# Every fourth expert row summed by VectorE in SBUF, and a new order in stick-breaking

## The chip, the core and the metric

The kernel runs on one core of one Trainium2 chip, as one program. The metric is the device time of one execution in microseconds; beside it stands the profile of one further execution. Five engines work side by side and wait for each other through semaphores: TensorE (PE, its weight loads PEld), VectorE (DVE), ScalarE (ACT), GpSimd (POOL), and SyncE (SP), which here only starts transfers. The gathers are started by POOL.

## The reference

One encoder layer over 1024 tokens of width 1024, float32 throughout. Two of its parts are touched.

Stick-breaking attention, 8 heads of width 64, strictly causal, in blocks of queries:

```python
z = jnp.einsum('bhtd,bhsd->bhts', qh[:, :, start:end], kh[:, :, :end])
mask = jnp.arange(end)[None, :] < jnp.arange(start, end)[:, None]
log_1m = jnp.where(mask, jax.nn.log_sigmoid(-z), 0.0)
suffix = lax.cumsum(log_1m, axis=3, reverse=True) - log_1m
a = jnp.where(mask, jnp.exp(jax.nn.log_sigmoid(z) + suffix), 0.0)
outs.append(jnp.einsum('bhts,bhsd->bhtd', a, vh[:, :, :end]))
```

PEER, a layer of 16384 single-neuron experts, of which each token takes 16 per head for 8 heads, so 128 rows of u and of v per token:

```python
ub = u[eb]
act = jax.nn.gelu(jnp.einsum('thkd,td->thk', ub, xb).astype(jnp.float32), approximate=False)
w = (gb * act).astype(xb.dtype)
return jnp.einsum('thk,thkd->td', w, v_emb[eb])
```

The result of PEER is added to the residual h, and a last RMSNorm gives the output.

## The kernel before

The program is a sequence of phases with barriers between them: input norm and projections, gated linear attention, stick-breaking, output projection, memory attention, key scores, and the expert phase, which takes two thirds of the time. Inside a phase the program is written out engine by engine, so the order of each engine's instructions is that of the code, and semaphores tie the engines together.

**Stick-breaking** (`stick_phase`). A tile is 128 keys by up to 512 queries, for one head. The list `work` says in which order the tiles are done, `(pair of heads, half of the queries, block of keys)`; `rounds` (L871) writes it for one pair, and an entry with -1 belongs to the pair before. Each entry gives two tiles, one per head. A tile on the diagonal has fewer queries and is masked. In iteration `i` the engines work on entries of different age: TensorE makes r for entry i - 2 (L1002, L1006: the suffix sums, by a triangular matrix and the carry), z for entry i (L1017), and the product with v for entry i - 3 (L1032) into `po`, which holds one half of the queries for one pair. ScalarE takes the exp of r for entry i - 2 (L934, into `aw`, shown as tok) and three passes over z of entry i (L941 to L943). VectorE makes the softplus `sps` (L958, shown as heads) and the carry (L976, L978), and four iterations after a pair's last entry of a half it copies `po` out as a high and a low part (L984, L136, into x_t) and so frees it: `o_free`. POOL masks diagonal tiles, `sps` and `aw`, both on L905.

**The expert phase** (`expert_phase`). Eight blocks of 128 tokens, one token per partition, and 128 expert rows per block. Row R is a gather (L1433) of 128 x 8 KB, u and v of one expert per token, into one of `ROWS` = 7 slots. Then VectorE takes the dot product of u with the normalised token (L1660), ScalarE makes the weight by Gelu and gate (L1774, L1775) and a diagonal matrix of it (L1778, 4 slots `dg`), TensorE adds diagonal times v to the PSUM accumulator of the block (L1905, two matmuls of 512 columns), and `row_used` frees the slot for row R + 7. Before a block's first row TensorE puts the residual H into the accumulator by a product with the identity (L1898). After a block's last row, during the first 16 rows of the next, VectorE works the final norm (`finish`, L1546 to L1569) in steps between the dot products, and SP stores the block. Between dot products VectorE also chooses the experts two groups ahead (`select`), and during the first 4 blocks all engines do memory attention and key scores for the second half of the tokens (`later`, by the table of class `Later`).

## Time and profile before

| | us |
|---|---|
| median of 3 runs | 3914.02 |
| lowest, highest | 3913.75, 3915.89 |
| the profiled execution, its own time | 3910.47 |
| span of its trace | 3908.7 |

| engine | busy us | share |
|---|---|---|
| PE | 3189.3 | 82% |
| DVE | 2324.4 | 59% |
| ACT | 1640.7 | 42% |
| POOL | 1596.6 | 41% |

The span is cut into 40 slices of 97.7 us each; a digit is the busy share of a slice in tenths. A row of a timeline gives start, duration, engine and line, what is written from what, and in brackets how long the engine sat idle before it and what it waited for. In a windows row the engines stand in the order PE, PEld, DVE, ACT, POOL, each with its busy time and in brackets the number of instructions, then the granted TensorE clock as a share of full speed, the busy share of the 16 DMA engines and the rate. The median time of the line's transfers "to landing" is from the issue until the data is there. A wait for several things is put down to the last. The shares are averages over phases with different limits.

### The profile page before, as it was taken

The page shows a single profiled execution, that of the slowest core. Times are in us where ns is not written, and L with a number is a line of the kernel's source. Part 1 is how long each engine was busy: PE and PEld are TensorE (multiplying, and loading weights), DVE is VectorE, ACT ScalarE, POOL GpSimd, SP SyncE. Part 2 cuts the span into 40 slices and gives each one's busy share as a digit, 9 for nine tenths or more (in the row PEclk, how much of TensorE's full clock was granted, in tenths as well). Part 3 has the DMA queues.
Part 4 walks back from the last instruction along what each step waited for, and adds up shares of the span by engine and source line. Part 5 has one row for each costly group of instructions (what it writes and reads, how often), then busy time and mean ns, then how long its engine had stood idle before and what let it go on. Part 6 is the DMA issues. An engine that isn't in the chain of part 4 may idle for free.

```text
span 3908.7 us, 35644 instructions
## 1 busy us (share of the span) xinstructions
PE 3189.3 (82%) x10072; PEld 1663.8 (43%) x10072; DVE 2324.4 (59%) x5493; ACT 1640.7 (42%) x4273; POOL 1596.6 (41%) x1176
## 2 busy tenths in 40 slices
PE   6798788977887888888888888888787777877777
PEld 5577533666666443434333444443222222222222
DVE  3343344234334777776776676676667667667665
ACT  2121377223222555544544444454444444444443
POOL 0000011000000556444555445445765766666765
PEclk8899899988988999999999999999999999999999
DMA  2101000221023999999999999999999999999998
GB/s 77 35 24 43 0 1 1 87 97 43 23 76 121 416 409 419 417 415 414 414 414 414 417 410 415 413 408 412 420 414 408 420 405 420 416 415 420 414 407 353
DMA packets 173010, 1147.66 MB, mean 294 GB/s; under 512 B 19472, under 2 KB 21536, under 8 KB 41632
## 3 DMA queue, kind: packets, MB, share of 16 engines
q0 software_dynamic: 147456, 1073.81, 66.8%
q1 hardware_dynamic: 25376, 71.87, 5.1%
q8 instruction: 64, 1.05, 0.1%
q14 instruction: 114, 0.93, 0.1%
HBM read 1141.41 MB, written 4.19 MB: 293 GB/s over the span
## 4 chain that ended last, share of the span: by engine, by line
DMA 29%; POOL 9%; PE 9%; issue 7%; ACT 7%; DVE 6%; POOLq 0%; ACTq 0%; DVEq 0%
DMA expert_rows<-in_uv,expert_index 29%; POOL expert_rows L1433 9%; PE expert_acc L1905 8%; DVE expert_rows L1660 4%; ACT expert_dg L1778 1%; ACT expert_wt L1775 1%; ACT L1774 1%; ACT expert_wt L1774 1%; ACT L1694 1%; DVE expert_w_lo L136 1%; ACT expert_w_hi L131 1%; DVE expert_hot L1523 0%; ACT expert_best L1694 0%; ACT L1720 0%; ACT expert_spare L1720 0%
## 5 line engine op out<-in xcount | busy, mean ns | idle before, releaser
L1905 PE MATMUL expert_acc<-expert_rows,expert_dg 128*128 128x512 f32 x4096 | 2010.6, 623 | 485.4 <-ACT expert_dg L1778 484.6
L1433 POOL DMA_INDIRECT expert_rows<-in_uv,expert_index x1024 | 1547.1, 1511 | 1094.2 <-PE expert_acc L1905 809.1
L1660 DVE CUSTOM_DVE_ANT_0 expert_rows<-expert_rows,expert_xn 128x1024 f32<-128x1024 f32 x1024 | 1254.8, 1225 | 719.5 <-DMA expert_rows<-in_uv,expert_index 716.3
L1905 PEld LDWEIGHTS expert_acc<-expert_rows,expert_dg 128*128 128x128 f32 x4096 | 737.6, 194 | 1606.4 <-ACT expert_dg L1778 1004.9
L1774 ACT ACTIVATE expert_wt<-expert_dot 128x1 f32<-128x1 f32 x1024 | 207.4, 203 | 1329.9 <-DVE expert_dot L1660 1327.6
L1778 ACT ACTIVATE expert_dg<-ident,expert_wt 128x128 f32<-128x128 f32 x1024 | 411.2, 402 | 33.7
L1775 ACT ACTIVATE expert_wt<-expert_wt,expert_gate 128x1 f32<-128x1 f32 x1024 | 301.3, 294 | 33.4
L1425 POOL IOTA expert_iota<- 128x16 f32 x1 | 0.1, 144 | 534.8 <-PEq L1793 534.8
L905 POOL TENSOR_SCALAR_AFFINE_SELECT heads<-heads 128x128 f32<-128x128 f32 x64 | 20.7, 324 | 331.6 <-DVE heads L958 331.3
L958 DVE SCALAR_TENSOR_TENSOR heads<-stick_pz,stick_t 128x512 f32<-128x512 f32 (+3 forms) x96 | 53.2, 557 | 134.0 <-ACT stick_t L943 133.8
L1774 ACT ACT_TABLE_LOAD x79 | 101.4, 1283 | 7.3 <-DVE expert_dot L1660 6.0
L142 PE MATMUL expert_side<-late_hi,expert_w_lo 128*128 128x512 f32 x128 | 103.6, 809 | 0.0
L1002 PE MATMUL stick_pz<-heads,negtri 128*128 128x512 f32 (+3 forms) x192 | 87.4, 545 | 0.9 <-POOL heads L905 0.9
L1660 DVE DVE_READ_ACCUMULATOR2_ANT expert_dot<- 128x1 f32 x1024 | 84.8, 83 | 0.0
L1694 ACT ACT_TABLE_LOAD x62 | 79.5, 1283 | 1.1
L136 DVE TENSOR_TENSOR expert_w_lo<-expert_w_raw,expert_w_hi 128x512 fp32r<-128x512 f32 x48 | 33.2, 693 | 74.5 <-ACT expert_w_hi L131 74.5
L1032 PE MATMUL stick_po<-tok 128*64 128x512 f32 (+3 forms) x192 | 43.7, 535 | 33.4 <-DVE x_t_lo L136 17.8
L1006 PE MATMUL stick_pz<-stick_carry,negone 128*128 128x512 f32 (+3 forms) x160 | 63.6, 481 | 0.0
L934 ACT ACTIVATE tok<-stick_pz 128x512 f32<-128x512 f32 (+3 forms) x96 | 43.6, 481 | 45.2 <-PE stick_pz L1006 44.9
L142 PE MATMUL keys_pq<-z_a_hi,pq_w_lo 128*128 128x512 f32 x128 | 51.9, 406 | 11.2 <-DMA keys_sk<-in_sub_keys 9.3
L487 POOL MEMSET decay_keep<- 128x1024 f32 x1 | 1.0, 951 | 142.1 <-POOLq L334 142.1
L142 PE MATMUL mixout_bank<-out_w_hi,x_t_lo 128*128 128x512 f32 x128 | 51.1, 400 | 7.5 <-DVE out_w_lo L136 7.5
(367 smaller groups left out, 4182.0 us busy)
## 6 DMA issues: line engine op xcount, KB each, us to landing
expert_rows<-in_uv,expert_index POOLq DMA_INDIRECT x1024, 12.4
H<-in_x SPq DMA_DIRECT2D x8, 1024.0 KB, 10.3
pq_w_raw<-in_w_pq SPq DMA_DIRECT2D x16, 512.0 KB, 3.3
expert_w_raw<-in_w_pq SPq DMA_DIRECT2D x32, 256.0 KB, 8.9
stick_w_raw<-in_w_feat SPq DMA_DIRECT2D x8, 512.0 KB, 3.3
tok_w_raw<-in_w_tok SPq DMA_DIRECT2D x8, 512.0 KB, 4.0
out_w_raw<-in_w_out SPq DMA_DIRECT2D x8, 512.0 KB, 5.3
mk_w_raw<-in_w_mk SPq DMA_DIRECT2D x8, 512.0 KB, 5.0
```

The source lines that it names most:

```text
L136: return nc.vector.tensor_tensor(lo, x, hi.bitcast(F32), ALU.subtract)
L142: nc.tensor.matmul(out, wl, xh, start=start, stop=False)
L958: nc.vector.scalar_tensor_tensor(sps[:, s, c0:], pz[s][:, c0:], 0.0, t[:, s, c0:], ALU.max, ALU.add).then_inc(sp_ready, 1)
L1002: last = nc.tensor.matmul(pz[s][:, c0:], negtri[:, :], sps[:, s, c0:], start=False, stop=(c1 == HALF), skip_group_check=True)
L1006: last = nc.tensor.matmul(pz[s][:, c1:], negone[:, :], carry[:, h, th, (k + 1) % 2, c1:], start=False, stop=True, skip_group_check=True)
L1433: pool.indirect_dma_start(out=rows[R % ROWS], out_offset=None, in_=uv, in_offset=bass.IndirectOffsetOnAxis(ap=index[:, q, r:r + 1], axis=0 ...
L1660: nc.vector.tensor_tensor_reduce(rows[R % ROWS][:, 0:D], rows[R % ROWS][:, 0:D], xn[:, :], 1.0, 0.0, ALU.mult, ALU.add, dot[:, h % 2, r:r ...
L1694: nc.scalar.activation(best[:, q, :], best[:, q, :], ACT.Exp, bias=small[:, 0, q:q + 1], accum_out=small[:, 1, q:q + 1]).then_inc(exp_read ...
L1774: link(nc.scalar.activation(wt[:, s, 0, r:r + 1], dot[:, s, r:r + 1], ACT.Gelu))
L1775: link(nc.scalar.activation(wt[:, s, 1, r:r + 1], wt[:, s, 0, r:r + 1], ACT.Copy, scale=gate[:, q, r:r + 1]))
L1778: nc.scalar.activation(dg[:, r % DG, :], co.ident[:, :], ACT.Copy, scale=wt[:, s, 1, r:r + 1]).then_inc(diag_ready, 1)
L1905: last_mm = nc.tensor.matmul(acc[:, h * HALF:(h + 1) * HALF], dg[:, r % DG, :], rows[(TOPK * (PH * b + g) + r) % ROWS][:, D + h * HALF:D + ...
```

## The change

Four edits. In the expert phase every fourth row (R mod 4 = 3, an own row) is no longer multiplied by a diagonal and summed in PSUM. VectorE multiplies it by its weight and adds it to `own_acc`, a buffer in SBUF, one row late: behind the dot product of the next row. The first own row of a block adds to H, so TensorE no longer puts H into the accumulator. POOL waits for `own_used` where the slot held an own row and for `row_used` otherwise, `finish` adds the two sums, and `cand` shares its memory with `hot`. In stick-breaking the entry (-1, 0, 1) moves from second to first place in `rounds`; POOL does the masks of `aw` of an iteration ahead of those of `sps`; and VectorE copies `po` out at the start of its iteration instead of the end.

```diff
--- before.py
+++ after.py
@@ -868,7 +868,7 @@
 
-    rounds = [(0, 1, 7), (-1, 0, 1), (0, 1, 6), (-1, 0, 0), (0, 1, 5), (0, 1, 4), (0, 0, 3), (0, 1, 3), (0, 0, 2),
+    rounds = [(-1, 0, 1), (0, 1, 7), (0, 1, 6), (-1, 0, 0), (0, 1, 5), (0, 1, 4), (0, 0, 3), (0, 1, 3), (0, 0, 2),
               (0, 1, 2), (0, 1, 1), (0, 1, 0)]
@@ -906,14 +906,14 @@
             for i in range(M + 2):
+                for n in (2 * i - 4, 2 * i - 3):
+                    if n >= 0 and diag[n]:
+                        pool.wait_ge(a_ready, n + 1)
+                        strict(aw[:, n % S, :], tile(n)[3], a_masked)
                 for m in (2 * i, 2 * i + 1):
                     if i < M and diag[m]:
                         pool.wait_ge(sp_ready, m + 1)
                         strict(sps[:, m % S, :], tile(m)[3], sp_masked)
-                for n in (2 * i - 4, 2 * i - 3):
-                    if n >= 0 and diag[n]:
-                        pool.wait_ge(a_ready, n + 1)
-                        strict(aw[:, n % S, :], tile(n)[3], a_masked)
 
@@ -948,6 +948,14 @@
             for i in range(M + 5):
+                n = 2 * (i - 4) + 1
+                if 0 <= n < N and tile(n)[2] == 0:
+                    pr, th, _, _ = tile(n)
+                    dve.wait_ge(pv_done, n + 1)
+                    hi, lo = (x[:, GLA_HEADS + pr, th * HALF:(th + 1) * HALF] for x in mix_t)
+                    nc.vector.tensor_copy(hi, po[th][:, :]).then_inc(hi_ready, 1)
+                    dve.wait_ge(hi_ready, ended.index((pr, th)) + 1)
+                    low(nc, lo, po[th][:, :], hi).then_inc(o_free, 1)
                 two = (2 * i, 2 * i + 1) if i < M else ()
@@ -976,14 +984,6 @@
                             nc.vector.tensor_copy(new[:, c0:c1], sps[:, s, c0:c1]).then_inc(carry_ready, 1)
-                n = 2 * (i - 4) + 1
-                if 0 <= n < N and tile(n)[2] == 0:
-                    pr, th, _, _ = tile(n)
-                    dve.wait_ge(pv_done, n + 1)
-                    hi, lo = (x[:, GLA_HEADS + pr, th * HALF:(th + 1) * HALF] for x in mix_t)
-                    nc.vector.tensor_copy(hi, po[th][:, :]).then_inc(hi_ready, 1)
-                    dve.wait_ge(hi_ready, ended.index((pr, th)) + 1)
-                    low(nc, lo, po[th][:, :], hi).then_inc(o_free, 1)
 
@@ -1296,6 +1296,21 @@
     E = 2 * D
+    OWN = 4
+
+    def own(R):
+
+        return R % OWN == OWN - 1
+
+    def own_rows(R):
+
+        return (R + 1) // OWN
+
+    def pe_rows(R):
+
+        return R + 1 - own_rows(R)
+
+    own_ready, own_used = sem("own_ready"), sem("own_used")
     landed = [sem(f"landed{j}") for j in range(ROWS)]
...
@@ -1541,13 +1560,14 @@
                 ms, var, tmp, y = (small2[:, j:j + 1] for j in range(4))
-                dve.wait_ge(row_used, TOPK * PH * (b + 1) + ROWS)
+                dve.wait_ge(row_used, pe_rows(TOPK * PH * (b + 1) - 1))
+                dve.wait_ge(own_used, own_rows(TOPK * PH * (b + 1) - 1))
                 dve.wait_ge(stored, 16 * (b + 1))
-                n = put(nc.vector.tensor_copy(hb[:, :], acc[:, :]))
+                n = put(nc.vector.tensor_tensor(hb[:, :], own_acc[:, :], acc[:, :], ALU.add))
                 yield
                 yield
                 have(n)
-                n = put(nc.vector.tensor_tensor_reduce(hb[:, :], hb[:, :], acc[:, :], 1.0, 0.0, ALU.mult, ALU.add, ms))
+                n = put(nc.vector.tensor_tensor_reduce(acc[:, :], hb[:, :], hb[:, :], 1.0, 0.0, ALU.mult, ALU.add, ms))
                 yield
...
@@ -1637,6 +1657,19 @@
 
+            def add_own(R):
+
+                b, r = divmod(R, TOPK * PH)
+                n = own_rows(R)
+                dve.wait_ge(own_ready, n)
+                if r > OWN:
+                    dve.wait_ge(own_used, n - 1)
+                    so_far = own_acc[:, :]
+                else:
+                    so_far = co.H[:, b, :]
+                nc.vector.scalar_tensor_tensor(own_acc[:, :], rows[R % ROWS][:, D:E], wt[:, R // TOPK % 2, 1, R % TOPK:R % TOPK + 1],
+                                               so_far, ALU.mult, ALU.add).then_inc(own_used, 1)
+
             def body(b, odd, more, last):
@@ -1659,6 +1692,8 @@
                                                        ALU.mult, ALU.add, dot[:, h % 2, r:r + 1]).then_inc(dots, 1)
+                        if R and own(R - 1):
+                            add_own(R - 1)
                         later(R)
...
@@ -1772,12 +1808,19 @@
                         link(nc.scalar.activation(wt[:, s, 0, r:r + 1], dot[:, s, r:r + 1], ACT.Gelu))
-                        link(nc.scalar.activation(wt[:, s, 1, r:r + 1], wt[:, s, 0, r:r + 1], ACT.Copy,
-                                                  scale=gate[:, q, r:r + 1]))
-                        act.wait_ge(row_used, TOPK * g + r + 1 + ROWS - DG)
-                        nc.scalar.activation(dg[:, r % DG, :], co.ident[:, :], ACT.Copy,
-                                             scale=wt[:, s, 1, r:r + 1]).then_inc(diag_ready, 1)
-                        later(TOPK * g + r)
+                        R = TOPK * g + r
+                        weight = nc.scalar.activation(wt[:, s, 1, r:r + 1], wt[:, s, 0, r:r + 1], ACT.Copy,
+                                                      scale=gate[:, q, r:r + 1])
+                        if own(R):
+                            weight.then_inc(own_ready, 1)
+                        else:
+                            link(weight)
+                            n = pe_rows(R) - 1
+                            if n >= DG:
+                                act.wait_ge(row_used, n - DG + 1)
+                            nc.scalar.activation(dg[:, n % DG, :], co.ident[:, :], ACT.Copy,
+                                                 scale=wt[:, s, 1, r:r + 1]).then_inc(diag_ready, 1)
+                        later(R)
 
...
@@ -1892,21 +1933,18 @@
                     pe.wait_ge(out_ready, b - 1)
-                if b == HB:
-                    pe.wait_ge(mo_added, 2 * HB)
-                for h in range(2):
-                    nc.tensor.matmul(acc[:, h * HALF:(h + 1) * HALF], co.ident[:, :],
-                                     co.H[:, ds(b, 1), h * HALF:(h + 1) * HALF].rearrange("p o d -> p (o d)"),
-                                     start=True, stop=False, skip_group_check=True)
                 for g in range(PH):
                     for r in range(TOPK):
-                        pe.wait_ge(diag_ready, TOPK * PH * b + (TOPK * g + r + 1))
-                        for h in range(2):
-                            last_mm = nc.tensor.matmul(acc[:, h * HALF:(h + 1) * HALF], dg[:, r % DG, :],
-                                                       rows[(TOPK * (PH * b + g) + r) % ROWS][:, D + h * HALF:D + (h + 1) * HALF],
-                                                       start=False, stop=False, skip_group_check=True)
-                        last_mm.then_inc(row_used, 1)
-                        later(TOPK * (PH * b + g) + r)
+                        R = TOPK * (PH * b + g) + r
+                        if not own(R):
+                            n = pe_rows(R) - 1
+                            pe.wait_ge(diag_ready, n + 1)
+                            for h in range(2):
+                                last_mm = nc.tensor.matmul(acc[:, h * HALF:(h + 1) * HALF], dg[:, n % DG, :],
+                                                           rows[R % ROWS][:, D + h * HALF:D + (h + 1) * HALF],
+                                                           start=not (g or r), stop=False, skip_group_check=True)
+                            last_mm.then_inc(row_used, 1)
+                        later(R)
```

VectorE where head pair 1 follows pair 0 in stick-breaking, before (CAST and the TENSOR_TENSOR behind it are the copy of `po`):

```order
L976 TENSOR_TENSOR stick_carry<-stick_carry,heads 128x128 [waits stick_carry_ready,stick_sp_masked,stick_r_full]
L978 COPY stick_carry<-heads 128x128
L958 SCALAR_TENSOR_TENSOR heads<-stick_pz,stick_t 128x512 [waits stick_logs,stick_carry_ready] x2
L984 CAST x_t_hi<-stick_po 128x512 [waits stick_pv_done]
L136 TENSOR_TENSOR x_t_lo<-stick_po,x_t_hi 128x512 [waits stick_hi_ready]
L958 SCALAR_TENSOR_TENSOR heads<-stick_pz,stick_t 128x384 [waits stick_logs,stick_carry_ready] x2
L976 TENSOR_TENSOR stick_carry<-stick_carry,heads 128x256 [waits stick_carry_ready,stick_sp_masked,stick_r_full]
```

and now:

```order
L984 TENSOR_TENSOR stick_carry<-stick_carry,heads 128x128 [waits stick_carry_ready,stick_sp_masked,stick_r_full]
L986 COPY stick_carry<-heads 128x128
L956 CAST x_t_hi<-stick_po 128x512 [waits stick_pv_done]
L136 TENSOR_TENSOR x_t_lo<-stick_po,x_t_hi 128x512 [waits stick_hi_ready]
L966 SCALAR_TENSOR_TENSOR heads<-stick_pz,stick_t 128x512 [waits stick_logs,stick_carry_ready] x2
L966 SCALAR_TENSOR_TENSOR heads<-stick_pz,stick_t 128x384 [waits stick_logs,stick_carry_ready] x2
L984 TENSOR_TENSOR stick_carry<-stick_carry,heads 128x256 [waits stick_carry_ready,stick_sp_masked,stick_r_full]
```

The copy stands ahead of the iteration's softplus instead of behind it; the lines are numbered 8 higher, and L956 is the old L984.

TensorE at the same place, before; the row that waits for stick_o_free is the new pair's first product into `po`:

```order
L1032 MATMUL stick_po<-tok 64x512 [waits stick_a_ready]
L1032 MATMUL stick_po<-tok 64x512
L1002 MATMUL stick_pz<-heads,negtri 128x384 [waits stick_sp_masked]
L1006 MATMUL stick_pz<-stick_carry,negone 128x256 [waits stick_carry_ready]
L1002 MATMUL stick_pz<-heads,negtri 128x384 [waits stick_sp_masked]
L1006 MATMUL stick_pz<-stick_carry,negone 128x256 [waits stick_carry_ready]
L1017 MATMUL stick_pz<-H 128x512 [waits stick_a_ready]
L1017 MATMUL stick_pz<-H 128x512
L1032 MATMUL stick_po<-tok 64x128 [waits stick_a_masked,stick_o_free]
L1032 MATMUL stick_po<-tok 64x128
```

and now:

```order
L1017 MATMUL stick_pz<-H 128x512 [waits stick_a_ready]
L1017 MATMUL stick_pz<-H 128x512
L1032 MATMUL stick_po<-tok 64x384 [waits stick_a_masked]
L1032 MATMUL stick_po<-tok 64x384
L1002 MATMUL stick_pz<-heads,negtri 128x256 [waits stick_sp_masked]
L1006 MATMUL stick_pz<-stick_carry,negone 128x128 [waits stick_carry_ready]
L1002 MATMUL stick_pz<-heads,negtri 128x256 [waits stick_sp_masked]
L1006 MATMUL stick_pz<-stick_carry,negone 128x128 [waits stick_carry_ready]
L1017 MATMUL stick_pz<-H 128x384 [waits stick_a_ready]
L1017 MATMUL stick_pz<-H 128x384
L1032 MATMUL stick_po<-tok 64x128 [waits stick_a_masked,stick_o_free]
L1032 MATMUL stick_po<-tok 64x128
```

Two products stand where one stood between the last of pair 0 (64x512) and the one that waits: that of the diagonal tile (0, 0, 1), 64x384, has gone ahead.

POOL's first masks of the phase, before (heads is `sps`, tok is `aw`):

```order
L905 AFFINE_SELECT heads<-heads 128x128 [waits stick_sp_ready] x6
L905 AFFINE_SELECT tok<-tok 128x128 [waits stick_a_ready] x2
L905 AFFINE_SELECT heads<-heads 128x128 [waits stick_sp_ready] x2
L905 AFFINE_SELECT tok<-tok 128x128 [waits stick_a_ready] x2
L905 AFFINE_SELECT heads<-heads 128x128 [waits stick_sp_ready] x2
L905 AFFINE_SELECT tok<-tok 128x128 [waits stick_a_ready] x4
```

and now:

```order
L905 AFFINE_SELECT heads<-heads 128x128 [waits stick_sp_ready] x4
L905 AFFINE_SELECT tok<-tok 128x128 [waits stick_a_ready] x2
L905 AFFINE_SELECT heads<-heads 128x128 [waits stick_sp_ready] x2
L905 AFFINE_SELECT tok<-tok 128x128 [waits stick_a_ready] x2
L905 AFFINE_SELECT heads<-heads 128x128 [waits stick_sp_ready] x2
L905 AFFINE_SELECT tok<-tok 128x128 [waits stick_a_ready] x2
```

The masks of `aw` come one iteration's pair earlier among those of `sps`.

VectorE in the expert phase, the middle of a group of rows, before (ISA is the dot product, in two parts):

```order
L1501 MAX expert_best<-expert_cand_rest 128x8
L1502 TENSOR_SCALAR expert_small<-expert_best 128x1
L1660 ISA expert_rows,expert_dot<-expert_rows,expert_xn 128x1024
L1660 ISA expert_dot 128x1
L1505 MAX_INDEX expert_best_j<-expert_best,expert_cand_rest 128x8
L1660 ISA expert_rows,expert_dot<-expert_rows,expert_xn 128x1024
L1660 ISA expert_dot 128x1
```

and now at the same step of the selection:

```order
L1693 ISA expert_rows,expert_dot<-expert_rows,expert_xn 128x1024
L1693 ISA expert_dot 128x1
L1670 SCALAR_TENSOR_TENSOR expert_own_acc<-expert_rows,expert_wt,expert_own_acc 128x1024
L1520 MAX expert_best<-expert_hot 128x8
L1521 TENSOR_SCALAR expert_small<-expert_best 128x1
L1693 ISA expert_rows,expert_dot<-expert_rows,expert_xn 128x1024
L1693 ISA expert_dot 128x1
L1524 MAX_INDEX expert_best_j<-expert_best,expert_hot 128x8
L1693 ISA expert_rows,expert_dot<-expert_rows,expert_xn 128x1024
```

The addition to own_acc stands behind the dot product of the row after and ahead of the step of the selection.

## Rows read from the trace of the kernel before

**Rows 1.** The page's slices, DMA share in tenths and GB/s, 40 equal slices.

```profile
DMA  2101000221023999999999999999999999999998
GB/s 77 35 24 43 0 1 1 87 97 43 23 76 121 416 409 419 417 415 414 414 414 414 417 410 415 413 408 412 420 414 408 420 405 420 416 415 420 414 407 353
```

**Rows 2.** Windows: stretch, length, busy PE, PEld, DVE, ACT, POOL, clock, DMA, GB/s.

```profile
1800.00:2000.00 200.00, 162.74 (x392) 70.28 (x393) 148.51 (x378) 105.47 (x287) 106.19 (x77) 0.98 1.01 416
3000.00:3200.00 200.00, 156.52 (x319) 54.84 (x317) 134.15 (x346) 86.87 (x262) 142.00 (x80) 0.99 1.01 416
```

**Rows 3.** The gather's line: durations in ns, starts, then issue to landing.

```profile
L1433 POOL DMA_INDIRECT expert_rows<-in_uv,expert_index x1024: 984/1495/2066, 1252.9 to 3883.0; - x171
...
DMA to landing us min/median/max: 6.0/12.4/15.5
```

**Rows 4.** Timeline of DVE at the end: start, duration, instruction, idle before.

```profile
3892.92 1.23 DVE L1660 CUSTOM_DVE_ANT_0 expert_rows<-expert_rows,expert_xn 128x1024 f32<-128x1024 f32 x1 [1.25 <-DMA expert_rows<-in_uv,expert_index]
...
3895.41 1.23 DVE L1660 CUSTOM_DVE_ANT_0 expert_rows<-expert_rows,expert_xn 128x1024 f32<-128x1024 f32 x1 [1.25 <-DMA expert_rows<-in_uv,expert_index]
...
3899.71 1.23 DVE L1546 COPY expert_hb<-expert_acc 128x1024 f32<-128x1024 f32 x1 [3.07 <-PE expert_acc L1905]
```

**Rows 5.** Waits in stick-breaking: us in total, times, longest.

```profile
ACT tok L934 <- PE stick_pz L1006: 44.9, 29, 4.5
...
PE stick_po L1032 <- DVE x_t_lo L136: 17.8, 3, 5.9
...
PE stick_po L1032 <- POOL tok L905: 15.5, 9, 2.7
```

**Rows 6.** Timeline where head pair 1 follows pair 0.

```profile
518.70 1.13 PE L1017 MATMUL stick_pz<-H 64*128 64x512 f32 x4
...
524.29 0.68 DVE L984 CAST x_t_hi<-stick_po 128x512 fp32r<-128x512 f32 x1
...
525.01 0.69 DVE L136 TENSOR_TENSOR x_t_lo<-stick_po,x_t_hi 128x512 fp32r<-128x512 f32 x1
...
525.76 0.69 PE L1032 MATMUL stick_po<-tok 128*64 128x128 f32 x4 [5.93 <-DVE x_t_lo L136]
...
528.13 0.38 ACT L934 ACTIVATE tok<-stick_pz 128x256 f32<-128x256 f32 x1 [4.54 <-PE stick_pz L1006]
```

**Rows 7.** Timeline at a later wait for a mask in the same pair.

```profile
540.11 0.85 ACT L934 ACTIVATE tok<-stick_pz 128x384 f32<-128x384 f32 x2
...
541.06 0.55 POOL L905 TENSOR_SCALAR_AFFINE_SELECT heads<-heads 128x128 f32<-128x128 f32 x1 [1.51 <-DVE heads L958]
...
541.57 0.85 POOL L905 TENSOR_SCALAR_AFFINE_SELECT tok<-tok 128x128 f32<-128x128 f32 x2
...
542.47 1.97 PE L1032 MATMUL stick_po<-tok 128*64 128x512 f32 x4 [2.67 <-POOL tok L905]
```

**Rows 8.** The page's groups: line, count, busy, mean ns, idle before.

```profile
L1905 PE MATMUL expert_acc<-expert_rows,expert_dg 128*128 128x512 f32 x4096 | 2010.6, 623 | 485.4 <-ACT expert_dg L1778 484.6
...
L1774 ACT ACTIVATE expert_wt<-expert_dot 128x1 f32<-128x1 f32 x1024 | 207.4, 203 | 1329.9 <-DVE expert_dot L1660 1327.6
...
L1778 ACT ACTIVATE expert_dg<-ident,expert_wt 128x128 f32<-128x128 f32 x1024 | 411.2, 402 | 33.7
...
L1775 ACT ACTIVATE expert_wt<-expert_wt,expert_gate 128x1 f32<-128x1 f32 x1024 | 301.3, 294 | 33.4
```

**Rows 9.** Groups from 1400 us on: the norm's last operation.

```profile
L1569 DVE SCALAR_TENSOR_TENSOR expert_hb<-expert_acc,expert_small,expert_gfinal 128x1024 f32<-128x1024 f32 x8 | 10.2, 1280 | 0.0
```

**Rows 10.** Waits of DVE over the first 16 rows of block 1.

```profile
DVE expert_rows L1660 <- DMA expert_rows<-in_uv,expert_index: 3.8, 6, 0.9
```

**Rows 11.** Timeline: a gather alone, and one issued during a dot product.

```profile
1255.64 0.99 POOL L1433 DMA_INDIRECT expert_rows<-in_uv,expert_index  x1 [0.30 <-issue]
...
3010.24 1.22 DVE L1660 CUSTOM_DVE_ANT_0 expert_rows<-expert_rows,expert_xn 128x1024 f32<-128x1024 f32 x1 [0.71 <-DMA expert_rows<-in_uv,expert_index]
...
3010.41 1.93 POOL L1433 DMA_INDIRECT expert_rows<-in_uv,expert_index  x1 [0.56 <-issue]
```

20 lines of the change are left out of this document (12 added, 8 removed).

## The prediction

> **What bounds the kernel now.** I read the page's slices first. From about 1250 us to the end the DMA digit is 9 and the GB/s row stands at 405 to 420 [rows 1]. That is the expert phase, two thirds of the span. The windows put numbers on it: 416 GB/s and a DMA share of 1.01 in a stretch that also carries the late attention and key scores (DVE busy 148.5 of 200 us, PE 162.7) and the same 416 GB/s in one that carries only expert rows (DVE 134.2, PE 156.5) [rows 2]. Engine load changes and the rate does not, so no engine sets it.
>
> The chain of waits can mislead here: it runs round the loop gather, dot product, weight, matmul, ring slot, next gather, and gives each a share. The end of the phase tells transfer from loop apart. The last gather is issued at 3883.0 [rows 3]; afterwards no slot matters, and the last dot products still start at 3892.92 and 3895.41, 2.49 us apart, each after 1.25 us of waiting for the DMA [rows 4]. So about five rows stand queued in the DMA, drained at one per 2.49 us; issue to landing is 12.4 us in the median against 6.0 at the least [rows 3]. Between landing and freeing a row needs only some 4.2 us (dot 1.23, weight and diagonal about 1, matmuls 2.0). The ring of 7 has slack: the DMA would starve only if a row came free some 12.4 - 6.0 = 6.4 us later than it does.
>
> The other 1250 us are phases bound by engines. The one touched is stick-breaking, 462 to 712 us. In its waits TensorE stands 17.8 us for x_t_lo in three places, up to 5.9 each, and 15.5 us for POOL's mask of the weights in nine; ScalarE stands 44.9 us for TensorE's r matmul [rows 5].
>
> **The change part by part.** Stick-breaking: output copy and rounds. In rows 6 TensorE starts its z matmul at 518.70 for 1.13 us, then may not write the next head pair's first product into po until VectorE has copied the finished pair out. That copy (0.68 + 0.69 us) stands at the end of VectorE's iteration, behind a softplus that needs three ScalarE passes over the tile whose z was only just made. It begins at 524.29 and TensorE goes on at 525.76: an idle 5.93 us. ScalarE then idles 4.54 us up to 528.13 [rows 6]. Afterwards VectorE copies first, which needs only a product one iteration older, and the tile (0, 0, 1) goes between the finished pair and the first tile of the next, so the buffer is asked for one iteration later. Both remove the same wait, 3 x 5.93 = 17.8 us [rows 5, 6]. The copies (1.37 us) now stand ahead of the softplus, hidden in VectorE's wait for ScalarE.
>
> Stick-breaking: mask order. POOL waits in program order, and the masks of a fresh tile stand ahead of those of weights ready earlier. In rows 7 the second exp ends at 540.96 (540.11 + 0.85), but POOL begins the sps mask at 541.06 and the aw pair at 541.57, which ends 542.42; TensorE goes on at 542.47 after 2.67 idle. Weights first, each mask (0.3 us) follows its exp and the second ends near 541.3: 1.1 us earlier, and the remaining 1.6 us are ScalarE's own. Nine waits at about 1 us give 9 us at most [rows 5, 7].
>
> The ceiling is 17.8 + 9 = 27 us, the floor near zero, because TensorE runs into what is late next: in the widest tiles TensorE and ScalarE are both nearly full, and narrow diagonal tiles leave short iterations where the chain z, three activations, softplus, mask, r needs two iterations. With x_t_lo gone, the next thing late is the exp that ScalarE owes; it had 4.54 us idle there to give, plus smaller gaps, 44.9 us in total [rows 5, 6]. I take the larger term almost whole (16 of 17.8) and half of the smaller (5 of 9): -21 us, with 10 and 27 as ends.
>
> Expert phase, removed: per own row (256 of 1024) four matmul pieces, 2010.6 / 1024 = 1.96 us of TensorE, some 500 of the 2010.6 us of L1905, and one ScalarE diagonal, 0.40 us; also the products that put H into the accumulator [rows 8]. TensorE has time to spare beside a bound DMA, so these are worth 0.
>
> Added: 256 times scalar_tensor_tensor over 128x1024. No row has it with three SBUF operands; with a PSUM input it takes 1.28 us [rows 9], and the dot product with two SBUF inputs 1.23 [rows 4]. I take 1.28, so 328 us of VectorE. In the densest window VectorE is busy 148.5 of 200 us and some 76 rows pass, 19 of them own: 148.5 + 24.3 = 173 of 200 [rows 2]. On average it fits, so 0. The tight place is a block's first 16 rows, where the normalisation of the block before is worked in: from 1588.7 to 1630.6 VectorE waits for landings only 3.8 us [rows 10], and four additions want 5.1. It is 1.3 us short there and catches up in the next group; of the 6.4 us of slack that is a fifth. I charge +1 us for all seven boundaries; had the queue no slack it would be 7 x 1.3 = 9.
>
> Moved: an own row is freed by VectorE after the next row's dot product, so not 4.2 but about 5.0 us after it landed (2.49 + 1.23 + 1.28). The add also waits for ScalarE's weight; that is 0.5 us of work after a dot 2.5 us before, so it is there unless ScalarE is changing tables. POOL waits for two semaphores in turn, with as many gathers as before; SP's transfers are the same. The first DMAs are not touched.
>
> The tail: today 3.07 us lie between the last dot and the copy of acc [rows 4]: 0.20 + 0.29 for the weight [rows 8], then diagonal and matmuls. Row 1023 is an own row, so it becomes 0.2 + 0.29 + 1.28 and four handoffs, about 1.85: -1.2 us. The sum of both halves takes the place of a copy of equal size.
>
> **A port that speaks against the change.** POOL's gather takes 0.98 us at the least and 2.07 at the most [rows 3], and the pattern is plain: the gather at 1255.64, before the first dot product, takes 0.99 and stands 0.30 behind the one before it; the one at 3010.41, issued 0.17 after a dot began at 3010.24, takes 1.93 and so ends 0.9 after the dot ended [rows 11]. A vector instruction with two SBUF operands holds POOL up until it ends. The new add is of that kind, so an own row may hold one gather up once more, by up to 1.28 us. The Trainium skill states the mechanism (SBUF — State Buffer, Who interferes with whom): a VectorE instruction with two SBUF inputs and a GpSimd instruction that reads SBUF exclude each other, and the later one blocks fully. The trace agrees, with 0.99 against 1.93. By the rule alone the sum would be that of rival 2.
>
> **The sum.** The profiled execution has a span of 3908.7 and a time of 3910.47. -21 + 0 + 1 - 1.2 = -21.2, so 3889.3. The median shown is 3914.02, 3.55 above it, which gives 3892.8; I say 3892.
>
> **The rivals.**
> 1. Stick-breaking gives back most of it. For it: ScalarE and TensorE alternate as the bound, and the reordered diagonal tiles stand two in a row, (1, 1, 7) and (1, 1, 6), so that a carry is asked for one iteration after it is made. Against it: both engines idle at the same place. A third of the 21 stays, -7: 3907.
> 2. VectorE or the port slows the expert loop: slower. Place: the gather's issue. Today a gather and its issue time fill about 2.5 us when a dot is in the way. If each own row held POOL 1.25 us more than it can make up, four rows would take 4 x 2.49 + 1.25 = 11.2 us and the phase 256 x 1.25 = 320 more: 4212. It decides once the queue in the DMA is used up, that is after five such rows without a catch-up. Against it: POOL issues a gather in 0.99 + 0.30 = 1.3 us when nothing is in the way [rows 11], so one unblocked gather in four repays one blocked twice. A weaker form, with catch-up only outside the 16 dense rows and the late attention, costs +20 to +60 net: about 3935.
> 3. The loop was a little short of slots after all. For it: 414 in some slices and 420 in others [rows 1]. If early freed slots and an idle TensorE brought all to 420, 1.2% of 2600 us, up to 30 us more would go: 3865. Against it: an own row is freed later, not earlier.
> 4. The change does not act where it should: the buffer wait in stick-breaking stays because the product before it is late too. The forecast would then be 3912, no change.
>
> **How the numbers follow.** Forecast 0.70; rival 1 0.10; rival 2 0.10, nearly all in its weak form; rival 3 0.06; rival 4 0.04. No change means within 0.2%, 7.8 us, about what a measurement of this kernel can tell. Faster: 0.70 + 0.06 + half of rival 1, and a little for rests, 0.82; same: the other half of rival 1 and rival 4, 0.08; slower 0.10. The forecast's own range is 3884 to 3905 (stick-breaking -27 to -10, boundaries 0 to +9 with small weight). For 8 in 10 I reach over rival 1 above and a little toward rival 3 below: 3878 to 3912.
>
> **What would show it.** In the profile after: the stick-breaking phase some 20 us shorter, no wait of TensorE for x_t_lo above 1 us, and POOL's mask waits for it down to half. In the expert phase 414 to 417 GB/s in every window, VectorE busy 80 to 87%, TensorE near 60 to 65%, landings 2.49 us apart, and issue to landing shorter than 12.4 us by about the time that slots come free later. The last dot to the end 1.2 us shorter. I am wrong if the GB/s falls below 410 in windows with own rows, if gathers of 2 us and more leave the landing median under 8 us, or if the stick-breaking phase shrinks by less than 10.

## The result, and the profile after

The changed kernel takes 3871.67 us in the median of 4 runs (3867.91 to 3874.54), beside 3914.23 for the kernel before on the same chip (3913.75 to 3915.89, 4 runs): a ratio of 0.989, 95% interval 0.9873 to 0.9907, so 42.6 us less. The prediction said 3892 and 3878 to 3912. The direction was right; the gain was twice the one forecast and the time lies below the range.

The profiled execution of the changed kernel took 3874.54, with a span of 3872.8, so the two spans differ by 35.9 us. That is less than the 42.6 of the medians, because the profiled execution after was the slowest of its four and the one before lay 3.8 us under its median; sizes of single terms below are those of the profiles. The slices after (DVE, granted clock, DMA share, GB/s):

```profile
DVE  3344354252336888887887887788787778778776
...
PEclk8799899979988999989899999999888899988889
DMA  1101000221125999999999999999999999999998
GB/s 76 33 27 44 0 1 17 87 93 33 44 81 215 419 413 417 413 411 410 418 418 412 408 416 410 415 406 414 416 405 420 414 407 420 413 413 417 411 411 355
```

The rates are those of [rows 1], but the expert phase begins earlier: slice 13 reads 215 where it read 121. Three lengths make up the whole difference. From the start of the first z product of stick-breaking to that of the last product into po: 245.2 us before (463.53 to 708.72), 204.5 after (464.86 to 669.39), so -40.7; what lies around it adds 1.0, and the first dot product of the expert phase starts at 1222.90 in place of 1262.61. From the first dot product to the last: 2632.8 before, 2637.6 after, +4.8. From the last dot product to the end: 13.3 and 12.3, -1.0. The gain is all in stick-breaking and the expert phase gave back a little.

Windows of stick-breaking (length, busy PE, PEld, DVE, ACT, POOL, clock), each one pair of heads long. Before:

```profile
512.36:576.12 63.76, 54.15 (x186) 22.80 (x188) 26.18 (x59) 45.16 (x97) 9.88 (x32) 0.92 0.00 1
576.12:637.33 61.21, 51.60 (x186) 22.25 (x188) 26.14 (x59) 45.07 (x97) 9.85 (x32) 0.94 0.00 1
```

After:

```profile
510.35:560.15 49.80, 49.70 (x186) 21.08 (x188) 25.98 (x60) 44.32 (x97) 9.98 (x32) 1.00 0.00 1
560.15:609.95 49.80, 49.70 (x186) 21.08 (x188) 25.95 (x60) 44.32 (x97) 9.96 (x32) 1.00 0.00 1
```

TensorE is busy 49.70 of 49.80 us: it is the bound and it is full. The same 186 matmuls also take less busy time, 49.70 in place of 54.15 and 51.60, with the granted clock at 1.00 instead of 0.92 and 0.94. Over the whole phase, before and after:

```profile
463.53:708.72 245.19, 210.84 (x732) 90.32 (x732) 103.16 (x230) 182.88 (x387) 39.48 (x128) 0.93 0.00 1
...
464.86:669.39 204.53, 202.39 (x732) 86.16 (x732) 102.56 (x230) 180.19 (x387) 39.87 (x128) 0.98 0.00 1
```

So the gain of 40.7 us has two parts: 8.5 us of TensorE's busy time, with the clock, and 32.2 us of its idle time (33.0 of waits for po, while small waits elsewhere grew by 0.8).

The waits over the phase after (total, times, longest), which answer to [rows 5]:

```profile
ACT tok L934 <- PE stick_pz L1006: 12.4, 15, 1.6
...
PEld stick_po L1032 <- DVE x_t_lo L136: 1.6, 3, 0.5
PEld stick_po L1032 <- POOL tok L905: 1.5, 2, 1.0
```

TensorE's 17.8 us for x_t_lo are gone (what is left is of the weight load, which runs beside a matmul) and of the 15.5 us for masks 0.3 are left. ScalarE's waits fell from 44.9 to 12.4. The timeline where pair 1 follows pair 0, which answers to [rows 6]:

```profile
518.57 0.68 DVE L956 CAST x_t_hi<-stick_po 128x512 fp32r<-128x512 f32 x1
519.28 0.69 DVE L136 TENSOR_TENSOR x_t_lo<-stick_po,x_t_hi 128x512 fp32r<-128x512 f32 x1
...
519.61 0.92 PE L1017 MATMUL stick_pz<-H 64*128 64x384 f32 x4
...
520.45 0.44 PE L1032 MATMUL stick_po<-tok 128*64 128x128 f32 x4
521.04 0.64 ACT L934 ACTIVATE tok<-stick_pz 128x256 f32<-128x256 f32 x2
```

The copy ends at 519.97, while TensorE is still busy with z, and the first product of the new pair follows at 520.45 with no idle time. ScalarE's exp at 521.04 has none either, where it stood 4.54 us.

The expert phase in windows, the two stretches of [rows 2]:

```profile
1800.00:2000.00 200.00, 137.05 (x294) 57.15 (x295) 172.40 (x400) 96.85 (x264) 104.13 (x78) 0.90 1.01 415
3000.00:3200.00 200.00, 134.05 (x240) 48.47 (x240) 156.41 (x368) 77.61 (x241) 120.96 (x80) 0.89 1.00 411
```

VectorE went from 148.5 to 172.4 us and from 134.2 to 156.4, about as computed. TensorE fell only to 137.05 and 134.05, while its granted clock fell from 0.98 and 0.99 to 0.90 and 0.89. The page's groups show the same, and the price of the new operation:

```profile
L1943 PE MATMUL expert_acc<-expert_rows,expert_dg 128*128 128x512 f32 x3072 | 1693.0, 690 | 782.5 <-ACT expert_dg L1821 779.9
L1452 POOL DMA_INDIRECT expert_rows<-in_uv,expert_index x1024 | 1481.1, 1446 | 1165.1 <-PE expert_acc L1943 685.6
L1693 DVE CUSTOM_DVE_ANT_0 expert_rows<-expert_rows,expert_xn 128x1024 f32<-128x1024 f32 x1024 | 1249.9, 1221 | 440.5 <-DMA expert_rows<-in_uv,expert_index 434.0
...
L1670 DVE SCALAR_TENSOR_TENSOR expert_own_acc<-expert_rows,expert_wt,expert_own_acc 128x1024 f32<-128x1024 f32 x248 | 317.6, 1281 | 7.4 <-ACT expert_wt L1812 7.4
```

The add takes 1281 ns with three SBUF operands (the 8 that add to H stand in another group), and it waited 7.4 us in all for a weight. The expert matmul's mean is 690 ns where it was 623. The gather's line, over the whole phase:

```profile
L1452 POOL DMA_INDIRECT expert_rows<-in_uv,expert_index x1024: 984/1488/2062, 1213.1 to 3848.1; - x171
```

Its durations are those of [rows 3], and its transfers land 11.9 us after the issue in the median, where it was 12.4.

### The profile page after: what moved, and what is told of

Same layout as the page of the kernel before. It is cut to its first block, busy times and chain, and to the rows that moved or that the text cites. A ratio compares the mean times of both kernels' runs of the same rounds, so it can differ in the third digit from the quotient of the medians.

```text
span 3872.8 us, 33523 instructions
## 1 busy us (share of the span) xinstructions
PE 2888.0 (75%) x9016; PEld 1540.9 (40%) x9016; DVE 2605.8 (67%) x5749; ACT 1536.0 (40%) x4017; POOL 1531.1 (40%) x1176
## 4 chain that ended last, share of the span: by engine, by line
DMA 34%; PE 11%; ACT 8%; DVE 8%; issue 6%; POOL 1%; POOLq 0%; DVEq 0%; ACTq 0%
DMA expert_rows<-in_uv,expert_index 34%; PE expert_acc L1943 10%; DVE expert_rows L1693 3%; ACT L1810 2%; DVE expert_own_acc L1670 2%; ACT L1730 2%; POOL expert_rows L1452 1%; ACT expert_wt L1812 1%; ACT expert_dg L1821 1%; ACT expert_wt L1810 1%; ACT expert_best L1730 1%; ACT L1756 0%; ACT expert_spare L1756 0%; DVE expert_dot L1693 0%; ACT expert_w_hi L131 0%
## 5 line engine op out<-in xcount | busy, mean ns | idle before, releaser
L1943 PE MATMUL expert_acc<-expert_rows,expert_dg 128*128 128x512 f32 x3072 | 1693.0, 690 | 782.5 <-ACT expert_dg L1821 779.9
L1452 POOL DMA_INDIRECT expert_rows<-in_uv,expert_index x1024 | 1481.1, 1446 | 1165.1 <-PE expert_acc L1943 685.6
L1943 PEld LDWEIGHTS expert_acc<-expert_rows,expert_dg 128*128 128x128 f32 x3072 | 614.3, 215 | 1733.6 <-ACT expert_dg L1821 1200.6
L1670 DVE SCALAR_TENSOR_TENSOR expert_own_acc<-expert_rows,expert_wt,expert_own_acc 128x1024 f32<-128x1024 f32 x248 | 317.6, 1281 | 7.4 <-ACT expert_wt L1812 7.4
L1821 ACT ACTIVATE expert_dg<-ident,expert_wt 128x128 f32<-128x128 f32 x768 | 308.4, 402 | 25.2
L136 DVE TENSOR_TENSOR expert_w_lo<-expert_w_raw,expert_w_hi 128x512 fp32r<-128x512 f32 x48 | 33.3, 694 | 71.0 <-ACT expert_w_hi L131 71.0
L142 PE MATMUL expert_side<-expert_w_hi,expert_o_lo 128*128 128x512 f32 x64 | 58.8, 919 | 0.0
L1244 DVE COPY scores<-keys_ps 128x512 f32 (+1 forms) x16 | 11.1, 692 | 70.9 <-PE keys_ps L1210 70.9
## 6 DMA issues: line engine op xcount, KB each, us to landing
expert_rows<-in_uv,expert_index POOLq DMA_INDIRECT x1024, 11.9
```

The costliest lines, as they stand in the source:

```text
L142: nc.tensor.matmul(out, wl, xh, start=start, stop=False)
L1452: pool.indirect_dma_start(out=rows[R % ROWS], out_offset=None, in_=uv, in_offset=bass.IndirectOffsetOnAxis(ap=index[:, q, r:r + 1], axis=0 ...
L1670: nc.vector.scalar_tensor_tensor(own_acc[:, :], rows[R % ROWS][:, D:E], wt[:, R // TOPK % 2, 1, R % TOPK:R % TOPK + 1], so_far, ALU.mult, ...
L1821: nc.scalar.activation(dg[:, n % DG, :], co.ident[:, :], ACT.Copy, scale=wt[:, s, 1, r:r + 1]).then_inc(diag_ready, 1)
L1943: last_mm = nc.tensor.matmul(acc[:, h * HALF:(h + 1) * HALF], dg[:, n % DG, :], rows[R % ROWS][:, D + h * HALF:D + (h + 1) * HALF], start= ...
```

## The experiments

All edits to stick-breaking are parts of the change, made to the kernel before. In the profiles I read three lengths: the phase (first z product to last po product), and TensorE's idle time in it for x_t_lo and for POOL's masks of aw. A ratio's interval is some 0.16% wide to either side, 6 us; smaller differences are read from the traces alone, one profiled execution of each kernel. The kernel before, against which each ratio stands, took 3910.47 in the comparison of s_copy, s_rounds, s_masks and s_copy_rounds, 3914.15 in that of s_all, x_own, own128 and after_again, and 3913.16 in the last four's.

**One edit at a time.** Copy of po first (s_copy):

```diff
             for i in range(M + 5):
+                n = 2 * (i - 4) + 1
+                if 0 <= n < N and tile(n)[2] == 0:
+                    pr, th, _, _ = tile(n)
...
+                    low(nc, lo, po[th][:, :], hi).then_inc(o_free, 1)
                 two = (2 * i, 2 * i + 1) if i < M else ()
...
-                n = 2 * (i - 4) + 1
-                if 0 <= n < N and tile(n)[2] == 0:
-                    pr, th, _, _ = tile(n)
...
```

> The kernel before with one edit: VectorE copies po out at the start of its iteration. Theory A (the waits of TensorE in stick-breaking go in full, and its clock rises because it no longer idles): the copy can begin only when VectorE has done the carries of the iteration before, about 520.4 in the old trace, and ends near 521.8 where TensorE asks at 519.8, so of each 5.93 us some 2 stay: 3 x 3.9 = 12 us plus some us of clock, -12 to -18. Theory B (each edit removes its wait alone and the next late thing takes the place): -6 or less. The mask waits: by A they shrink too, since ScalarE is no longer in arrears after the stall, from 15.5 to about 10; by B they stay at 15.5.

The new order of tiles (s_rounds):

```diff
-    rounds = [(0, 1, 7), (-1, 0, 1), (0, 1, 6), (-1, 0, 0), (0, 1, 5), (0, 1, 4), (0, 0, 3), (0, 1, 3), (0, 0, 2),
+    rounds = [(-1, 0, 1), (0, 1, 7), (0, 1, 6), (-1, 0, 0), (0, 1, 5), (0, 1, 4), (0, 0, 3), (0, 1, 3), (0, 0, 2),
```

With it one product into po, that of the diagonal tile (0, 0, 1), stands between the last of pair 0 and the one that waits for the buffer, where none stood before.

> The kernel before with one edit: the entry (-1, 0, 1) first in rounds. Theory A: the new pair's first product is asked for one iteration, about 4 us, later, while the copy still ends behind the softplus; about 1 to 2 us of each 5.93 stay, so -12 to -20 with the clock. Theory B: -6 or less, x_t_lo wait replaced by another of TensorE.

Masks of aw first (s_masks):

```diff
             for i in range(M + 2):
+                for n in (2 * i - 4, 2 * i - 3):
+                    if n >= 0 and diag[n]:
+                        pool.wait_ge(a_ready, n + 1)
+                        strict(aw[:, n % S, :], tile(n)[3], a_masked)
                 for m in (2 * i, 2 * i + 1):
...
-                for n in (2 * i - 4, 2 * i - 3):
```

> The kernel before with one edit: POOL masks the weights first. Theory A (much of the mask waits are an echo of the stall before them, in which ScalarE fell behind): of 15.5 us go the 4 us at the start and about 1 us each of the other six, -8 to -11, the 5.9 us waits for x_t_lo stay three times. Theory B (the order alone makes the waits): all 15.5 go, -15 or more.

**Edits together.** Copy and rounds, without the masks (s_copy_rounds):

> The kernel before with both edits for the buffer wait, masks as before. Theory A: no wait for x_t_lo, 17.8 us gone, and the clock near full in these stretches, so -22 to -28; mask waits down to 6 to 10 us. Theory B: x_t_lo wait gone but the mask waits grow by what was hidden behind it, above 20 us, total -10 or less.

All three, expert phase as before (s_all):

> The kernel before with the three edits in stick-breaking and none in the expert phase. Theory A: the whole gain is here, -40 to -44 us, stick-breaking 205 to 207 us long. Rival: the expert edit carries part of the gain, then this gives -25 or so.

The two other pairs, run later, complete the set (s_masks_copy and s_masks_rounds; the edits are those above):

> Two of the three edits in stick-breaking: weights masked first and po copied out first, rounds as before; expert phase as before. The copy alone left 5.9 us of TensorE waiting for x_t_lo and 14.0 for the masks, the masks alone left 17.8 and 0.3. Theory A, the three edits do one job together and the order of rounds is needed because the copy is late without it: a wait for x_t_lo of about 6 us in three places stays, the mask waits are gone, so 6 us idle in place of 0.3 with all three, a phase near 211 us, about 3876. Theory B, two of them are enough because the iteration that was late is on time once the masks come early: no wait above 0.5 us, 3868 to 3871, as with all three.

> Weights masked first and the new order of rounds, po copied out at the end as before; expert phase as before. Rounds alone left 4.4 us for x_t_lo and 17.9 for the masks. Theory A: 4 to 5 us for x_t_lo stay, masks 0.3, phase near 209, about 3875. Theory B, two are enough: no wait above 0.5 us and 3868 to 3871. A third outcome, that the masks' gain of 15 us is used up by the new order as the copy's was, would give 3890.

Measured, each against the runs of the kernel before in the same comparison:

| edits | median us | ratio (95%) | phase | idle, x_t_lo | idle, masks |
|---|---|---|---|---|---|
| none (before) | 3914.23 | 1 | 245.2 | 17.8 | 15.5 |
| copy | 3890.96 | 0.9949 (0.9932-0.9965) | 227.2 | 5.9 | 14.0 |
| rounds | 3895.54 | 0.9958 (0.9944-0.9972) | 231.1 | 4.4 | 17.9 |
| masks | 3890.50 | 0.9952 (0.9936-0.9969) | 227.5 | 17.8 | 0.3 |
| copy, rounds | 3893.72 | 0.9956 (0.9939-0.9972) | 233.1 | 0 | 20.1 |
| masks, copy | 3875.41 | 0.9899 (0.9883-0.9916) | 213.1 | 5.9 | 0.3 |
| masks, rounds | 3880.45 | 0.9914 (0.9897-0.9930) | 217.0 | 8.4 | 0.3 |
| all three | 3868.52 | 0.9884 (0.9868-0.9900) | 204.5 | 0 | 0.3 |

The waits of TensorE for po, over 462 to 712 us, on which the table rests. With the masks alone:

```profile
PE stick_po L1032 <- DVE x_t_lo L136: 17.8, 3, 5.9
```

With the copy and the rounds:

```profile
PE stick_po L1032 <- POOL tok L905: 20.1, 15, 2.7
```

With the rounds alone:

```profile
PE stick_po L1032 <- POOL tok L905: 17.9, 12, 2.7
...
PE stick_po L1032 <- DVE x_t_lo L136: 4.4, 3, 1.5
```

Against the expectations: s_copy came at -19.5 us for theory A's -12 to -18, but its mask waits stayed as theory B said; s_rounds at -14.9, in A's range; s_masks at -20, theory B. s_copy_rounds lay between its theories: the mask waits grew above 20 us as B said, and the time fell by 16.8 us, where A had 22 to 28 and B 10 or less. s_all at -45.7 and 204.5 us is theory A, a little past its ends.

Four things follow. First, the mask order alone takes away the mask waits, all but 0.3 of 15.5 us, while the copy alone leaves them (14.0, with the longest still 2.7): they are no echo of the stall for the buffer, and ScalarE has no share in them. The price is small: TensorE's waits for the masks of sps went from 0.9 to 1.9 us, with 0.6 for VectorE's softplus.

Second, without the masks the rounds add nothing to the copy. The waits for po are 19.9 us with the copy and 20.1 with both: what goes for x_t_lo (5.9) comes back for the masks (14.0 to 20.1), as TensorE comes earlier. The medians, 0.9949 and 0.9956, can't be told apart. The phase of s_copy_rounds is still 5.9 us longer in its trace, and that is busy time at a lower clock, not waiting. The phase of s_copy, then of s_copy_rounds:

```profile
465.25:692.46 227.21, 206.32 (x733) 87.73 (x733) 103.10 (x230) 182.47 (x387) 39.49 (x128) 0.96 0.00 1
...
464.23:697.33 233.10, 211.95 (x733) 89.42 (x733) 103.10 (x230) 182.63 (x387) 39.48 (x128) 0.93 0.00 1
```

It is the outcome of which rival 1 of the prediction spoke, in part, and it comes when the masks are left out; but what gives the time back is POOL's masks, and not ScalarE or a late carry.

Third, with the masks first nothing takes a wait's place: of the 18.1 us that the masks leave, the copy takes 11.9, the rounds take 9.4 and both take 17.8. Fourth, none of the three can be spared: copy without rounds leaves 5.9 us, rounds without copy 8.4, as the theories that called for all three expected; the theory that two are enough fell in both runs. The wait that stays under the old copy, 8.4 us, is larger than the 4 to 5 expected, and the time with it, 3880 in place of 3875.

Why the mask waits went wholly stands in the timeline of s_masks, at the place of [rows 7]:

```profile
530.11 0.58 ACT L934 ACTIVATE tok<-stick_pz 128x512 f32<-128x512 f32 x1
...
531.18 0.60 ACT L934 ACTIVATE tok<-stick_pz 128x512 f32<-128x512 f32 x1 [0.49 <-PE stick_pz L1006]
531.33 0.29 POOL L905 TENSOR_SCALAR_AFFINE_SELECT tok<-tok 128x128 f32<-128x128 f32 x1
...
531.84 0.33 POOL L905 TENSOR_SCALAR_AFFINE_SELECT tok<-tok 128x128 f32<-128x128 f32 x1 [0.23 <-ACT tok L934]
...
535.42 1.08 PE L1032 MATMUL stick_po<-tok 128*64 128x512 f32 x4
535.81 0.85 ACT L934 ACTIVATE tok<-stick_pz 128x384 f32<-128x384 f32 x2
```

The product of the 512 wide tile starts at 535.42, ahead of the 384 wide exps at 535.81. So it never needed those exps: it multiplies the weights of an iteration before, whose exps ended at 530.69 and 531.78. In the kernel before the same exps are these:

```profile
533.98 0.60 ACT L934 ACTIVATE tok<-stick_pz 128x512 f32<-128x512 f32 x1
...
535.48 0.60 ACT L934 ACTIVATE tok<-stick_pz 128x512 f32<-128x512 f32 x1 [0.91 <-PE stick_pz L1006]
```

They were ready at 536.08, and their masks ran at 541.57 [rows 7], 5.5 us late, only because POOL stood at the sps mask of a younger tile. Weights first, they would have ended near 536.4, three us ahead of TensorE's first look at 539.80.

**The expert half alone** (x_own: the changed kernel with the stick-breaking of before; the diff is the change without the three edits above).

> The expert edit alone, stick-breaking as before. Theory A (the gathers bound the phase, VectorE is tight only in the first rows of a block): the tail -1.2 and the loop +3 to +6 as the two traces differ by 4.8 between first and last dot product: +1 to +5 in all. Rival: an idle TensorE and an earlier weight help the loop, -5 or more.

Measured: 3921.05 (3914.35 to 3924.53, 11 runs), ratio 1.0016, interval 1.0007 to 1.0026: slower by 6 us. The trace splits the profiled execution's excess (span 3919.4 against 3908.7): the expert phase is 3.0 us longer than before (2635.8), and stick-breaking is 6.2 us longer (251.4) though its code is the old one and its waits for po are the old ones (over 462 to 712 us; the phase lasts until 717, and over the whole of it the masks' waits are 15.3 us in 9):

```profile
PE stick_po L1032 <- DVE x_t_lo L136: 17.8, 3, 5.9
PE stick_po L1032 <- POOL tok L905: 15.0, 8, 2.7
```

What lies around the two is 2.5 us longer and the tail 1.0 shorter. So at most half of this execution's excess is the own rows'; that of stick-breaking is busy time of TensorE, 217.3 us in place of 210.8, at a granted clock of 0.90 in place of 0.93 (see the last section). By medians of one comparison, own rows in every fourth place cost 6.9 us with the old stick-breaking (3921.05 against 3914.15), a little more than the +1 to +5 expected, and 4.6 with the new (after_again below, 3873.13 against 3868.52). The rival, a gain of 5 us or more, fell.

**How many own rows.** Four kernels with the three edits in place. One own row in 128 (own128), the changed kernel itself a second time (after_again), one in 8 (own8), and one in 4 with the addition issued twice, the first into the u half of the row's slot, which is free by then (own_twice).

```diff
-    OWN = 4
+    OWN = 128
```

own8 has 8 there.

> The changed kernel with one own row per block, the last, instead of every fourth. Theory A: keeps the shorter tail (-1.2) and takes no VectorE time inside the blocks, so 2 to 5 us faster than the changed kernel: 3866 to 3869. Rival (own rows cost the loop nothing, the 4.8 us between the traces is scatter): same as the changed kernel within 2 us.

> The changed kernel once more, for comparison on the same chip: 3868 to 3875.

> The changed kernel with every eighth row as own row, 128 in place of 256; the rows 127 stay own rows, so the short tail stays. All own rows off but one in 128 was 3866.2, every fourth 3871.7 to 3873.1. Theory A, the cost goes with the number of own rows: half of 7 us, 3869 to 3870. Theory B, the cost comes only when VectorE runs short in the dense rows, and with two own rows in 16 in place of four it does not: 3866 to 3867. Theory C, the cost has nothing to do with VectorE: 3872.

```diff
                 n = own_rows(R)
...
+                dve.wait_ge(dots, R + 1)
+                nc.vector.scalar_tensor_tensor(rows[R % ROWS][:, 0:D], rows[R % ROWS][:, D:E],
+                                               wt[:, R // TOPK % 2, 1, R % TOPK:R % TOPK + 1],
+                                               so_far, ALU.mult, ALU.add).then_inc(own_junked, 1)
+                dve.wait_ge(own_junked, n)
...
```

> The changed kernel with the own row's operation issued twice, the first time into the u half of the row's slot, which is free by then; the result is the same. VectorE does 256 more operations of 1.28 us, 328 us. In 1800:2000 it was busy 172.4 of 200 us, so it would be 172 + 24 = 197 there, and 156 + 25 = 181 in 3000:3200. Theory A, VectorE's time is cover and only the dense stretches have none left: the windows after 2600 us keep 410 to 418 GB/s and the first half loses a few per cent at most, 3875 to 3900. Theory B, each such operation costs the gather a fixed price through the port: the price of the edit, 4.6 us for 256 operations, is doubled everywhere, 3878, with the rate a little lower in every window. Theory C, the slots: an own row is freed 1.28 us later, still under the 6.4 us of slack, so no cost at all: 3873.

| additions by VectorE | median us | ratio (95%) | first to last dot product | gather behind 1223 us, mean ns |
|---|---|---|---|---|
| 0 (s_all) | 3868.52 | 0.9884 (0.9868-0.9900) | 2630.5 | 1527 |
| 8 (own128) | 3866.20 | 0.9878 (0.9862-0.9893) | 2630.3 | 1540 |
| 128 (own8) | 3870.14 | 0.9884 (0.9868-0.9901) | 2633.7 | 1489 |
| 256 (the change) | 3871.67 | 0.9890 (0.9873-0.9907) | 2637.6 | 1449 |
| 256 (after_again) | 3873.13 | 0.9898 (0.9882-0.9914) | 2636.2 | 1442 |
| 512 (own_twice) | 3901.84 | 0.9967 (0.9955-0.9980) | 2664.2 | 1371 |

The price is small up to 256 additions, some 5 us in the traces, and steep after: 27 to 28 us for the next 256. In the eight kernels without own rows the loop takes 2628.5 to 2632.8 us, so the scatter is 4 us. The three with 256 additions, 2637.6, 2636.2 and 2635.8 (x_own), lie above all of these, by 5 us in the mean. In one comparison on one chip the four executions of s_all (3866.90 to 3869.21) and the four of own128 (3864.53 to 3866.31) all lie under those of after_again (3872.24 to 3876.03), so a cost is there. Whether half the own rows cost half of it is not shown: 2633.7 for own8 is 0.9 above the scatter, and its median lies between the others. The time is what the theory of a price per own row expected (3869 to 3870), but the theories were only 2 us apart.

The windows say where own_twice loses. With it:

```profile
1300.00:1629.00 329.00, 234.54 (x608) 108.79 (x606) 299.89 (x656) 155.13 (x433) 168.12 (x124) 0.91 0.99 395
...
3029.00:3529.00 500.00, 335.42 (x592) 120.05 (x591) 452.51 (x977) 198.87 (x605) 268.62 (x197) 0.88 1.01 414
```

With the change:

```profile
1300.00:1629.00 329.00, 243.56 (x626) 113.40 (x625) 276.44 (x652) 162.54 (x452) 187.60 (x128) 0.92 1.01 415
...
3029.00:3529.00 500.00, 330.19 (x588) 119.75 (x588) 393.12 (x921) 201.49 (x607) 308.47 (x197) 0.89 1.01 414
```

In the stretch that carries the late attention the rate falls from 415 to 395 GB/s with VectorE at 91%. In the late one it stays at 414 with VectorE at 452.5 of 500 us, also 90%, so the share alone doesn't decide. What differs is the waiting that is left. In the first stretch VectorE waited for landings 73.4 us in s_all, 36.1 with the change and 5.5 with own_twice, where it also waited 11.7 for ScalarE's weights. In the late one it waited 159.0, 105.5 and 42.6. So the additions use up the time in which VectorE waits for rows, and where that is gone the rate falls. Blocks 0 to 3 took 23.8 us more than with the change, blocks 4 to 7 took 2.9 more. Block 0 took 12.2 of it, the first 24 rows of blocks 1 to 7 took 19.4 (455.4 us in place of 436.0), and their other rows won back some 5. The expectation's upper end, 3900, was just missed. A fixed price through the port (3878) and none at all (3873) both fell.

own128 is the best of all: 3866.20, 5.5 us under the changed kernel by the medians, in intervals that overlap, and 6.9 under after_again in the same comparison, with no overlap of the executions. It keeps the short tail and pays next to nothing in the loop. So the change's expert half, as it stands, is a loss of some 5 us, and its gain is stick-breaking's alone.

## Why the prediction was right or wrong

**The sum's large term, stick-breaking (-21): right mechanism, half its size.** The phase became 40.7 us shorter. Term by term: the buffer wait gave 17.8 where 16 were taken, the masks 15.2 where 5 were taken, and TensorE's busy time 8.5 where nothing was; small waits elsewhere took back 0.8. The miss of 19.7 us is thus mostly the masks (10.2) and the clock (8.5). Three steps failed.

- The masks, "the remaining 1.6 us are ScalarE's own. Nine waits at about 1 us give 9 us at most". Wrong: 15.2 of the 15.5 us went. I paired the masks at 541.57 with the exps at 540.11 because they stand next to each other in time; they belonged to the exps of 533.98 and 535.48. The code says so: ScalarE makes the weights of entry i - 2 and TensorE multiplies entry i - 3. This also made the ceiling too low: not 27 but 33.3 us, all of TensorE's idle time for po in [rows 5].
- The discount, "TensorE runs into what is late next", by which I took 21 of 27. With all three edits nothing was late next; TensorE is full to 49.70 of 49.80 us. Where the masks stay as they were, it is right in kind: the copy and rounds together gained nothing over the copy. The answer to what is late next stood in the list of waits: it was the masks, and the change took them away as well.
- The clock was left out. With the waits the granted clock stood at 0.93 over a phase that TensorE bounds, and with them filled at 0.98. A window over the phase before shows the first number; an estimate of 210.8 x 0.07, some 15 us at the most, was to be had from it, and 8.5 came.

**The buffer wait (16 of 17.8): right.** 17.8 came. But "both remove the same wait" was too simple: either edit alone leaves 5.9 or 4.4 us, and it takes both to make it zero. The copies did hide in VectorE's waits: where pair 1 follows pair 0 TensorE has no idle time behind them.

**Expert loop (0), block boundaries (+1): too low by some 4 us.** Together 4.8 us came in the profile of the change, 3.4 in that of after_again, and 5.7 to 7.1 against s_all. VectorE's 328 us are there (248 of 1281 ns and 8 more), 172.4 us in the dense window against 173 computed, no wait for ScalarE's weights worth naming. The cost is spread, 1 to 2 us or nothing in each block. The first 24 rows of blocks 1 to 7 hold only 1.0 of it (435.0 in s_all, 436.0 with the change), and among the kernels without own rows they vary from 434.4 to 436.1, so my +1 for the boundaries can be neither confirmed nor refused. My 0 for the rest is some 4 us short. The cause stays open: VectorE's time is one candidate, but with the own rows the granted clock fell too (0.95 over the span without, 0.93 in own8, 0.90 with 256), and the expert matmul's mean rose from 623 to 690 ns, so the other rows' slots can have come free later. No run parts the two.

**The slack of the ring: it held.** 6.4 us of slack stood against an own row that is free some 0.8 us later, and the landing median fell by 0.5, to 11.9. In own_twice the row is free another 1.28 us later and the late window still keeps its rate.

**The port, rival 2: not the price.** In the changed kernel the gather's median is 1.49 us as before, its range stays 0.98 to 2.06 (one gather of after_again takes 3.08), and its mean is lower the more additions there are from 128 on (the last column above). A gather that starts during an addition can wait for its end:

```profile
2683.26 1.28 DVE L1670 SCALAR_TENSOR_TENSOR expert_own_acc<-expert_rows,expert_wt,expert_own_acc 128x1024 f32<-128x1024 f32 x1
2683.39 2.01 POOL L1452 DMA_INDIRECT expert_rows<-in_uv,expert_index  x1 [0.72 <-PE expert_acc L1943]
```

It ends 0.86 us behind the addition, as a gather that starts during a dot product ends 0.86 behind that in the median. But that is rare: of the 1024 gathers 55 start during an addition, 708 during a dot product (683 before). And a gather waits for a slot more often than for the port: POOL stood idle 1165.1 us ahead of gathers. The rule of the Trainium skill (SBUF — State Buffer, Who interferes with whom), by which an addition with two inputs in SBUF and a gather block each other, agrees with the single instruction. Had each of the 256 additions held up a gather that POOL could not make up, the loop would have been 320 us longer; the trace shows that it does not reach the end of the loop while POOL has such idle time. The strong form of rival 2 fell; of the weak form the sign was right and 5 to 7 us came where 20 to 60 were said. own_twice, with 512 additions, shows where a cost of the weak form's size begins. There VectorE has hardly any waiting for landings left in the first stretch (5.5 of 329 us), while the mean gather is shorter still.

**The tail (-1.2): right.** -1.0 in the change. The chain is the one foreseen:

```profile
3860.52 1.22 DVE L1693 CUSTOM_DVE_ANT_0 expert_rows<-expert_rows,expert_xn 128x1024 f32<-128x1024 f32 x1 [1.26 <-DMA expert_rows<-in_uv,expert_index]
...
3861.79 0.20 ACT L1810 ACTIVATE expert_wt<-expert_dot 128x1 f32<-128x1 f32 x1 [1.52 <-DVE expert_dot L1693]
3862.02 0.29 ACT L1812 ACTIVATE expert_wt<-expert_wt,expert_gate 128x1 f32<-128x1 f32 x1
...
3862.35 1.28 DVE L1670 SCALAR_TENSOR_TENSOR expert_own_acc<-expert_rows,expert_wt,expert_own_acc 128x1024 f32<-128x1024 f32 x1 [0.60 <-ACT expert_wt L1812]
3863.72 1.22 DVE L1566 TENSOR_TENSOR expert_hb<-expert_own_acc,expert_acc 128x1024 f32<-128x1024 f32 x1
```

From the end of the dot product to the sum of both halves lie 1.98 us (3863.72 - 3861.74), for which 1.85 was computed and where 3.07 lay before [rows 4].

**The other rivals.** Rival 1 (stick-breaking gives it back) did not come; something like it came in s_copy_rounds, through POOL's masks and not through the engines that it named. Rival 3 (the loop short of slots, 3865) gave nearly the right time for a wrong reason: the loop became no faster. Rival 4 fell.

**What would show it.** As foretold: no wait for x_t_lo of TensorE, the landing median shorter (11.9 against 12.4), the tail, and VectorE nearly (78 to 86% for 80 to 87). Not as foretold: the masks' waits went to nothing and not to half, the phase shrank by 40.7 and not 20, TensorE stands at 67 to 69% and not 60 to 65, with its clock lower, and single windows read 411 GB/s.

## What to carry to other kernels

Pair a waiting instruction with the one it needs by the program's indices, not by what stands beside it in the timeline; a mask that runs right behind an exp may have been due 5 us earlier. When one in-order engine serves a young and an old tile, serve the old one first: here it removed every wait of its kind but 0.3 us, cost under 2 us of other waits, and let the other two edits count together. In a phase bound by TensorE count its idle time as the ceiling, ask of each next wait whether the same change removes it too, and add a term for the clock.

## What the runs showed of the hardware

**A filled TensorE holds its clock.** In the six profiles with all three edits the stick-breaking phase takes 204.3 to 204.5 us. The granted clock is at the lower of its two levels (1.2 and 2.4 GHz) until 471 to 475 us in them, and at 1.00 from there to the end of the phase. With waits left in it the phase varies: the kernel before and x_own have the same code there and the same waits, and 245.2 and 251.4 us, so the 8.5 us of the clock are the size in this pair of profiles and not a fixed one. Each later stretch at the lower level lies behind a wait of TensorE or reaches into one; not each wait of 2 to 3 us is followed by one. The z product of the 384 wide tile behind the stall shows what it costs. Before, behind 5.93 us of idle time, with the granted clock of the stretch:

```profile
529.24 1.65 PE L1017 MATMUL stick_pz<-H 64*128 64x384 f32 x4
...
525.10:531.80 6.70, 6.04 (x20) 3.37 (x20) 0.60 (x1) 1.61 (x4) 0.13 (x1) 0.50 0.00 0
```

In s_masks, behind the same stall of 5.92 us:

```profile
522.69 0.69 PE L1032 MATMUL stick_po<-tok 128*64 128x128 f32 x4 [5.92 <-DVE x_t_lo L136]
...
526.16 0.92 PE L1017 MATMUL stick_pz<-H 64*128 64x384 f32 x4
...
519.40:526.00 6.60, 3.31 (x12) 2.57 (x12) 2.08 (x4) 1.47 (x3) 0.88 (x3) 0.50 0.00 0
526.10:527.10 1.00, 1.00 (x7) 0.39 (x8) 0.00 (x0) 0.38 (x1) 0.29 (x1) 1.00 0.00 0
```

1.65 us against 0.92, near the ratio of the two levels. Both traces have the fall, and it lasts as long; in s_masks it began earlier against the stall, half of it passed while TensorE stood idle, and it was over when this product came. In the expert phase the rate shows no fall with the clock: TensorE lost a quarter of its matmuls there, its clock went from 0.98 to 0.90, and the windows keep 411 to 415 GB/s.

**The gather grows shorter under a busier VectorE.** Its mean is 1510 to 1540 ns with no or 8 additions, 1489 with 128, 1449 and 1442 with 256 and 1371 with 512, though each addition can block one. The traces say where it comes from: gathers that start during a dot product take 1763 ns in the mean before, 1593 with the change and 1463 in own_twice, so they start later in it. Why they do was not tested.
